# The opening block of a two-layer kernel: one list for its input transfers, and a new place for four weight slots

## Chip, cores and metric

One NeuronCore of one Trainium2 chip. The metric is the device time of one execution in microseconds (us); the profile is one execution of its own.

## The reference, cut to what matters

The reference is two blocks one after the other on 1024 tokens of width 1024, float32. Only its beginning is touched:

```python
c_act = jax.nn.silu(c)
mod = c_act @ ada_w[l] + ada_b[l]                       # 1024 x 6144: sh1, sc1, gt1, sh2, sc2, gt2
h = rms_norm(x, pre1_w[l]) * (1.0 + sc1) + sh1          # norm over the width, for each token
z = h @ w_in[l]                                         # the mixer's projections
...
mem_kv = mem @ w_mem_kv[layer]                          # second block, 256 memory rows, two layers
```

`mem_kv` depends on nothing but inputs, so the kernel computes it in its opening block and puts it into device memory for the second block.

## The kernel before, in words

**Layout.** Activations lie with the width on the 128 partitions, in 8 tiles, and the tokens along the free dimension, in two halves of 512. Each float32 operand of a large product is split into a rounded part (`hi`, fp32r) and the rest (`lo`), and a product is three matmuls (`three`, L285 to L292): w_hi x_hi, w_hi x_lo, w_lo x_hi.

**Weights.** All large weights come as one stream of slots of 128 x 1024 float32 (0.52 MB), in the order of use. A slot is fetched by SP into one of two raw buffers (`raw_w`, `RAW` = 2), rounded on ScalarE (`round_slot`, L268, the instruction L273) and its low part made on GpSimd (`rest_of_slot`, L276, L282) into one of four ring places (`w_hi`, `w_lo`, `RING` = 4). Slot n can be fetched when slot n - 2 has been split (semaphore `w_split`), and rounded when the matmuls of slot n - 4 are done.

**The opening block** (L975 to L1266) runs these parts side by side:

- `modulation` (L993): loads the vectors `vec` and constants `cst`, then 16 slots of `ada_w` (0.52 MB each, 6 buffers, so slot n waits for `ada_done` of slot n - 6). On the tensor engine each takes 8 matmuls (`modulate`, L943). After every four slots the vector engine picks the sums (`pick_group`, L950, L953); after the last it adds the bias and folds the norm's weight in (`folded`, L957).
- `first_slots` (L1041): fetches weight slots 0 to 13, rounds slots 0 to 3 and splits slots 0 to 11.
- `squares` (L1060): loads x in four quarters of 1.05 MB (first the two of token half 0), squares each tile on ScalarE (L1080) and adds them up on the vector engine (L1090).
- `statistic` (L807), once for each half: a reduction over the partitions on the tensor engine (L824), the root on ScalarE (L856), reciprocal (L850) and diagonal (L835) on the vector engine, and a matmul that spreads the factors (L831).
- `normed` (L1094), once for each half: scales x by norm and fold (vector engine, L1105), adds the shift and rounds (ScalarE, L1121, L1124, L1127), and makes the low parts on the vector engine (L1111) and GpSimd (L1136). Its result is H, high and low.
- `memory_keys` (L1150): loads the memory (`memT`, 1.05 MB), splits it (L1198, L1224), forms keys and values of two layers with weight slots 0 to 7 (24 matmuls each), copies them out of PSUM (keys on ScalarE L1204 and L1205, values on the vector engine L1232) and stores them (L1159, L1160). On ScalarE it also rounds slots 4 to 11, each behind the copy of the slot whose ring place it takes. `memT` and its parts lie in the space of H's low part, so the first low tiles of H wait for all eight slots (`kv_t` at 8).
- `heads_in` (`dense`, L607): the first projections from H, weight slots 8 to 12: four outputs for token half 0, the same four for half 1, and a fifth for both; 240 matmuls of 512 columns.

**What sets the order.** Each part is a set of generators, one for each engine; before every piece of work a generator yields a planned time. `ordered` (L137) merges the generators of an engine by these times, and the engine then executes all pieces in that order, each with its semaphore waits: a piece that waits holds everything behind it on its engine. All transfers are issued by SP. The planned times of the old kernel are fixed lines: S(n) = 12 + 2.2 n for modulation slot n, X(i) = 4 + 8 i for quarter i of x, K(n) = 15 + 3.2 n for slot n of the keys and values, N0 = S(16) + 2 for the fold (L988 to L991).

Of the kernel before, what the change touches and what calls it, by code (L numbers as in the profile page):

```python
# [20 lines left out]
F32 = mybir.dt.float32  # L21
# [138 lines left out]
def build(nc, a):  # L160
    ctx = ExitStack()
    with ctx:
# [811 lines left out]
        with ExitStack() as scope:  # L974
# [13 lines left out]
            S = lambda n: 12.0 + 2.2 * n  # L988
            X = lambda i: 4.0 + 8.0 * i
            K = lambda n: 15.0 + 3.2 * n  # L990
            N0 = S(ADA_EARLY) + 2.0  # L991

            def modulation():  # L993
                def on_sp(sp):
                    yield -10.0
                    sp.dma_start(vec[:], a["vec"]).then_inc(loaded.sem, 16)
                    sp.dma_start(cst[:], a["cst"]).then_inc(loaded.sem, 16)
                    for n in range(ADA_EARLY):
                        yield S(n - ADA_RING) + 1.0
                        if n >= ADA_RING:  # L1000
                            sp.wait_ge(ada_done.sem, n - ADA_RING + 1)
                        sp.dma_start(ada_w[:, n % ADA_RING].rearrange("p k m -> p (k m)"), a["ada"][n]
                                     ).then_inc(ada_full[n % ADA_RING].sem, 16)

                def on_pe(pe):
                    for n in range(ADA_EARLY):
                        yield S(n)
# [7 lines left out]
                def on_act(act, link):  # L1015
# [3 lines left out]
                    yield N0  # L1019
# [3 lines left out]
                def on_dve(dve, link):  # L1023
# [5 lines left out]
                    for g in range(ADA_EARLY // 4):  # L1029
                        yield S(4 * g + 4) + 0.6  # L1030
# [8 lines left out]
            split_at = lambda n: 10.5 + 2.6 * n if n < RING else K(n - RING) + 4.6  # L1039

            def first_slots():  # L1041
                def on_sp(sp):
                    for n in range(RING + 8 + RAW):
                        yield -3.0 + 0.1 * n if n < RAW else split_at(n - RAW) + 2.6
                        if n >= RAW:
                            sp.wait_ge(w_split.sem, n - RAW + 1)
                        sp.dma_start(raw_w[:, n % RAW], a["w"][n]).then_inc(w_full[n % RAW].sem, 16)

                def on_act(act, link):
                    for n in range(RING):  # L1050
                        yield split_at(n) - 1.4
                        round_slot(act, None, n, 0)

                def on_pool(pool, link):
                    for n in range(RING + 8):
                        yield split_at(n)
# [3 lines left out]
            def squares():  # L1060
# [3 lines left out]
                def on_sp(sp):  # L1064
                    for i in range(4):
                        yield X(i)
                        where = slice(4 * (i % 2), 4 * (i % 2) + 4), tokens(i // 2)
                        sp.dma_start(x0[:, where[0], where[1]], a["x"][:, where[0], where[1]]).then_inc(x_s[i].sem, 16)

# [4007 lines left out]
```

## Time and profile before

| | us |
|---|---|
| median of 3 runs | 3120.64 |
| lowest and highest | 3118.84, 3120.82 |
| the profiled execution | 3119.04 |
| its span, first to last instruction | 3117.2 |

Some 1.8 us of the profiled execution lie outside its span. The profile's page counts TensorE busy for 2885.4 us (93% of the span), VectorE 1606.1, ScalarE 1065.2 and GpSimd 1037.7. The opening block and its projections are the first 4.4% of the span; the row of busy tenths begins with 6 there, against 9 in nearly all slices behind it.

How to read it: in a timeline each line is one instruction, or several alike (x4) with the time from the first's start to the last's end; in brackets stands how long the engine had been idle and which work released it. PE is TensorE, DVE VectorE, ACT ScalarE, POOL GpSimd. SPq lines are the issues of transfers; such a line ends when it is issued, not when the data has landed.

### The profile page before, as it was taken

How to read it: one execution, taken by the hardware profiler on the slowest of the kernel's cores; microseconds unless marked ns; L12 is line 12 of the kernel's file. 1: busy time of each engine (PE TensorE's matmuls, PEld its weight loads, DVE VectorE, ACT ScalarE, POOL GpSimd, SP SyncE). 2: the span in 40 equal slices, each digit the busy share in tenths (PEclk: the TensorE clock that was granted, in tenths of full speed). 3: DMA queues.
4: the chain of work that ended last, by engine and by line, in shares of the span. 5: the costliest groups of instructions: out<-in, count | busy, mean ns of one | idle time of the engine just before them, and what ended most of it. 6: DMA issues, size and time to landing. Idle time of an engine off the chain costs nothing. (4 is left out here: it accounts for less than half of the span.)

```text
span 3117.2 us, 34782 instructions
## 1 busy us (share of the span) xinstructions
PE 2885.4 (93%) x14150; PEld 2181.5 (70%) x14150; DVE 1606.1 (52%) x1686; ACT 1065.2 (34%) x1474; POOL 1037.7 (33%) x577
## 2 busy tenths in 40 slices
PE   6999999999997989799999999899899998999887
PEld 5777777777775568577888777677566666777555
DVE  4263012325335352665555499633466673749557
ACT  4242222212216122433333344434433441347313
POOL 3232111113432121345555467432233331343102
PEclk8989999999998989899999999999999999999889
DMA  8111114662113343212222653412300002121201
GB/s 300 41 55 55 55 68 135 199 206 82 55 68 129 122 144 119 81 48 87 80 80 81 216 170 129 156 58 75 132 21 21 21 18 78 61 81 34 98 14 55
DMA packets 87618, 290.55 MB, mean 93 GB/s; under 512 B 9009, under 2 KB 13505, under 8 KB 86305
## 3 DMA queue, kind: packets, MB, share of 16 engines
q1 hardware_dynamic: 87458, 288.33, 27.5%
q8 instruction: 112, 1.84, 0.2%
q14 instruction: 48, 0.39, 0.0%
HBM read 223.70 MB, written 64.59 MB: 92 GB/s over the span
## 5 line engine op out<-in xcount | busy, mean ns | idle before, releaser
L282 POOL TENSOR_TENSOR w_lo_sb<-raw_w_sb,w_hi_sb 128x1024 fp32r<-128x1024 f32 x155 | 386.1, 2492 | 1241.2 <-ACT w_hi_sb L273 1241.1
L290 PE MATMUL ps<-h_hi_sb,w_hi_sb 128*128 128x512 f32 x720 | 300.4, 417 | 10.2 <-PEq L537 5.4
L290 PE MATMUL ps<-h_lo_sb,w_hi_sb 128*128 128x512 f32 x720 | 289.4, 402 | 0.0
L290 PE MATMUL ps<-h_hi_sb,w_lo_sb 128*128 128x512 f32 x720 | 251.9, 402 | 0.0
L273 ACT ACTIVATE w_hi_sb<-raw_w_sb 128x1024 fp32r<-128x1024 f32 x155 | 163.3, 1054 | 206.3 <-PE ps L290 155.2
L290 PE MATMUL ps<-z_lo,w_hi_sb 128*128 128x512 f32 x512 | 205.0, 400 | 0.0
L290 PE MATMUL ps<-merged_parts_hi_sb,w_hi_sb 128*128 128x512 f32 x472 | 190.8, 404 | 13.1 <-DVE merged_parts_lo_sb L2775 8.1
L290 PE MATMUL ps<-merged_parts_lo_sb,w_hi_sb 128*128 128x512 f32 x472 | 188.6, 399 | 0.0
L290 PEld LDWEIGHTS ps<-h_hi_sb,w_hi_sb 128*128 128x128 f32 x720 | 138.4, 192 | 55.4 <-issue 22.5
L290 PE MATMUL ps<-merged_parts_hi_sb,w_lo_sb 128*128 128x512 f32 x472 | 176.8, 396 | 0.0
L290 PE MATMUL ps<-z_hi,w_hi_sb 128*128 128x512 f32 x384 | 162.6, 423 | 13.9 <-PEq L912 5.6
L290 PEld LDWEIGHTS ps<-h_hi_sb,w_lo_sb 128*128 128x128 f32 x720 | 138.5, 192 | 34.1
L290 PEld LDWEIGHTS ps<-h_lo_sb,w_hi_sb 128*128 128x128 f32 x720 | 138.8, 193 | 31.2 <-issue 1.0
L290 PE MATMUL ps<-hid_hi_sb,w_hi_sb 128*128 128x512 f32 x308 | 124.2, 403 | 14.6 <-DVE hid_lo_sb L3311 14.6
L290 PE MATMUL ps<-z_hi,w_lo_sb 128*128 128x512 f32 x384 | 133.4, 402 | 0.0
L290 PE MATMUL ps<-h_hi,w_hi_sb 128*128 128x512 f32 x256 | 113.3, 443 | 14.9 <-POOL h_lo L3480 11.6
L3718 PE MATMUL ps<-att_p_t_sb,vh_sb 128*128 128x512 f32 (+3 forms) x288 | 124.2, 513 | 1.6 <-ACT att_p_t_sb L3852 1.6
L3032 POOL TENSOR_TENSOR w_lo_sb<-ffn_weight_sums_sb,w_hi_sb 128x512 fp32r<-128x512 f32 x72 | 105.2, 1465 | 55.3 <-ACT w_hi_sb L2986 55.1
L290 PE MATMUL ps<-hid_hi_sb,w_lo_sb 128*128 128x512 f32 x308 | 122.9, 399 | 0.0
L290 PE MATMUL ps<-hid_lo_sb,w_hi_sb 128*128 128x512 f32 x308 | 122.0, 396 | 0.0
L290 PEld LDWEIGHTS ps<-merged_parts_hi_sb,w_hi_sb 128*128 128x128 f32 x472 | 89.3, 189 | 42.7 <-issue 7.3
L290 PE MATMUL ps<-y_parts_hi_sb,w_hi_sb 128*128 128x512 f32 x224 | 97.6, 436 | 22.4 <-DVE y_parts_lo_sb L2283 8.9
(676 smaller groups left out, 6791.5 us busy)
## 6 DMA issues: line engine op xcount, KB each, us to landing
raw_w_sb<-in_w SPq DMA_DIRECT2D x237, 512.0 KB, 3.6
ada_late_sb<-in_ada SPq DMA_DIRECT2D x32, 512.0 KB
inbox_sb<-gates_out SPq DMA_DIRECT2D x24, 512.0 KB, 4.1
ffn_hidden_out<-ffn_hidden_box_sb SPq DMA_DIRECT2D x22, 512.0 KB, 6.2
ffn_hidden_sb<-ffn_hidden_out SPq DMA_DIRECT2D x20, 512.0 KB, 5.3
ada_w<-in_ada SPq DMA_DIRECT2D x16, 512.0 KB, 8.4
gates_out<-outbox_sb SPq DMA_DIRECT2D x16, 512.0 KB, 2.6
inbox_sb<-sums_out SPq DMA_DIRECT2D x16, 512.0 KB, 5.1
```

The lines of the kernel that those rows point to most:

```text
L273: nc.scalar.activation(w_hi[:, n % RING].rearrange("p t m -> p (t m)"), raw_w[:, n % RAW], ACT.Copy).then_inc(w_rounded.sem, 1)
L282: nc.gpsimd.tensor_tensor(w_lo[:, n % RING].rearrange("p t m -> p (t m)"), raw_w[:, n % RAW], flat_hi, ALU.subtract).then_inc(w_split.sem, 1)
L290: mm = nc.tensor.matmul(o, wt, xs, start=start and part == 0 and xs is x_hi, stop=stop and part == 1, skip_group_check=again)
L3032: nc.gpsimd.tensor_tensor(flat4(half_slot(w_lo, j)), weight_of(g, j), flat4(half_slot(w_hi, j)).bitcast(F32), ALU.subtract).then_inc(split ...
L3718: nc.tensor.matmul(ps[:, 6 + t, lo - HALF * t:HALF], v_of(u, s), pr[n % PR][:, 0:hi - lo], start=(s == 0), stop=(s == last(t))).then_inc(p ...
```

## The change

The planned times come from one list. Each of its 31 transfers is planned to land when the megabytes up to it have passed at 0.39 MB per us, and SP issues it 12 us before that. In the list slots 0 to 7 come early, most of x and the modulation behind them. The lines for S, K, the splits, the fold and the projections are worked out from these landing times. Weight slots 8 to 13 are not in the list: they stay in `first_slots`, at planned times worked out from `split_at`. The roundings of slots 4 to 11 move from `memory_keys` to `first_slots` with planned times of their own, and the wait on `kv_t` with them. The stores of keys and values get later planned times. `memT` gets a buffer of its own, and its two parts move behind the first four low tiles of H, so that the wait for `kv_t` at 8 stands at the low tiles 4 and 5.

```diff
-            S = lambda n: 12.0 + 2.2 * n
-            X = lambda i: 4.0 + 8.0 * i
-            K = lambda n: 15.0 + 3.2 * n
-            N0 = S(ADA_EARLY) + 2.0
+            MB_US = 0.39
+            fetched = [("vec", 0), ("cst", 0), ("w", 0), ("w", 1), ("mem", 0), ("ada", 0), ("w", 2), ("ada", 1), ("w", 3),
+                       ("x", 0), ("w", 4), ("ada", 2), ("w", 5), ("ada", 3), ("ada", 4), ("w", 6), ("ada", 5), ("w", 7),
+                       ("x", 1), ("ada", 6), ("ada", 7), ("x", 2), ("ada", 8), ("ada", 9), ("ada", 10), ("x", 3),
+                       ("ada", 11), ("ada", 12), ("ada", 13), ("ada", 14), ("ada", 15)]
+            megabytes = {"vec": 0.15, "cst": 0.6, "w": 0.524, "mem": 1.05, "ada": 0.524, "x": 1.05}
+            lands, now = {}, 0.0
+            for what, n in fetched:
+                now += megabytes[what] / MB_US
+                lands[(what, n)] = now
+            S, at = [], 0.0
+            for n in range(ADA_EARLY):
+                at = max(lands[("ada", n)] + 0.5, at + 1.3)
+                S.append(at)
+            X = lambda i: lands[("x", i)]
+            K, at = [], 13.0
+            for n in range(8):
+                at = max(lands[("w", n)] + 4.0, at)
+                K.append(at)
+                at += 3.2
+            K.append(at)
+            FOLDED = S[-1] + 4.0
+            H0 = FOLDED + 5.0
...
                 def on_sp(sp):
-                    yield -10.0
...
+                    for what, n in fetched:
+                        yield lands[(what, n)] - 12.0
...
+                        if what == "w":
+                            if n >= RAW:
+                                sp.wait_ge(w_split.sem, n - RAW + 1)
+                            sp.dma_start(raw_w[:, n % RAW], a["w"][n]).then_inc(w_full[n % RAW].sem, 16)
...
-            split_at = lambda n: 10.5 + 2.6 * n if n < RING else K(n - RING) + 4.6
+            split_at = []
+            for n in range(RING + 8):
+                ready = (lands[("w", n)] if n < 8 else split_at[n - RAW] + 4.5) + 1.5
+                split_at.append(max(ready, K[n - RING + 1] + 1.6) if n >= RING else ready)

             def first_slots():
                 def on_sp(sp):
-                    for n in range(RING + 8 + RAW):
-                        yield -3.0 + 0.1 * n if n < RAW else split_at(n - RAW) + 2.6
-                        if n >= RAW:
-                            sp.wait_ge(w_split.sem, n - RAW + 1)
+                    for n in range(8, RING + 8 + RAW):
+                        yield split_at[n - RAW] + 2.6
+                        sp.wait_ge(w_split.sem, n - RAW + 1)
                         sp.dma_start(raw_w[:, n % RAW], a["w"][n]).then_inc(w_full[n % RAW].sem, 16)

                 def on_act(act, link):
-                    for n in range(RING):
-                        yield split_at(n) - 1.4
+                    for n in range(RING + 8):
+                        yield split_at[n] - 1.4
+                        if n >= RING:
+                            act.wait_ge(kv_t.sem, n - RING + 1)
                         round_slot(act, None, n, 0)
...
-                        yield X(i) + 7.0 + 0.8 * (t % 4)
+                        yield X(i) + 0.6 + 1.0 * (t % 4)
...
-                            if n == 2:
+                            if n == 6:
                                 dve.wait_ge(kv_t.sem, 8)
...
-            memT = sb_over("mem_in", [P, DT, MEM], F32, h_lo_at)
-            MT = (sb_over("mem_parts_hi", [P, DT, MEM], F32R, h_lo_at + 8 * T),
-                  sb_over("mem_parts_lo", [P, DT, MEM], F32R, h_lo_at + 16 * T))
+            memT = sb_in(scope, "mem_in", [P, DT, MEM])
+            MT = (sb_over("mem_parts_hi", [P, DT, MEM], F32R, h_lo_at + 16 * T),
+                  sb_over("mem_parts_lo", [P, DT, MEM], F32R, h_lo_at + 24 * T))
...
-                        yield K(4 * layer + 4) + 3.0
+                        yield K[4 * layer + 4] + (22.0 if layer == 0 else 10.0)
...
                             n = 4 * layer + m
-                            yield K(n + 1) + 0.2
+                            yield K[n] + 3.4
                             act.wait_ge(kv_t.sem, n + 1)
...
-                            round_slot(act, None, n + RING, 0)
...
-                at = X(2 * h + 1) + 12.0
+                at = X(2 * h + 1) + 6.0
```

## Rows read from the trace of the kernel before

**Rows 1.** The page's first line, and SP's longest wait of 0 to 85 us (in total, times, longest).

```profile
span 3117.2 us, 34782 instructions
...
SPq L1047 <- POOL w_lo_sb L282: 38.6, 10, 6.6
```

**Rows 2.** Windows: length, PE, PEld, DVE, ACT, POOL busy (instructions), TensorE clock, DMA share, GB/s.

```profile
3.00:10.00 7.00, 0.00 (x0) 0.00 (x0) 3.55 (x6) 0.21 (x1) 0.00 (x0) 1.00 0.99 406
...
40.00:50.00 10.00, 10.00 (x89) 9.67 (x90) 5.05 (x9) 5.96 (x9) 7.30 (x3) 0.78 0.57 179
50.00:60.00 10.00, 10.00 (x122) 8.37 (x121) 1.82 (x4) 2.57 (x5) 2.10 (x2) 1.00 1.01 377
```

**Rows 3.** Timeline of SP: start us, us, what.

```profile
46.98 0.44 SPq L1068 DMA_DIRECT2D x_sb<-in_x  x1
...
48.68 0.44 SPq L1047 DMA_DIRECT2D raw_w_sb<-in_w  x1
```

**Rows 4.** The tile raw_w: splits on POOL, and DMA issue to landing.

```profile
L282 POOL TENSOR_TENSOR w_lo_sb<-raw_w_sb,w_hi_sb x12: 2338/2357/2652, 11.7 to 70.8; 128x1024 fp32r<-128x1024 f32 x12
...
DMA to landing us min/median/max: 3.5/5.1/11.8
```

**Rows 5.** Timeline of ACT (roundings L273, squares L1080, key copies L1204).

```profile
10.23 0.42 ACT L1198 ACTIVATE mem_parts_hi<-mem_in 128x256 fp32r<-128x256 f32 x1 [4.93 <-DMA mem_in<-in_mem]
...
56.85 1.06 ACT L273 ACTIVATE w_hi_sb<-raw_w_sb 128x1024 fp32r<-128x1024 f32 x1 [5.99 <-DMA raw_w_sb<-in_w]
57.94 0.38 ACT L1204 ACTIVATE mem_k_sb<-ps 64x256 f32<-64x256 f32 x1
...
61.97 1.06 ACT L273 ACTIVATE w_hi_sb<-raw_w_sb 128x1024 fp32r<-128x1024 f32 x1 [3.26 <-DMA raw_w_sb<-in_w]
62.93 0.61 ACT L1080 ACTIVATE norm_sq_sb<-x_sb 128x512 f32<-128x512 f32 x1
...
67.36 1.04 ACT L273 ACTIVATE w_hi_sb<-raw_w_sb 128x1024 fp32r<-128x1024 f32 x1
```

**Rows 6.** Timeline of DVE (diagonal L835, sums L1090, pick L950, scaling L1105, low part L1111).

```profile
45.18 1.25 DVE L835 TENSOR_TENSOR norm_diag_sb<-cst_sb,norm_stat_sb 128x512 f32<-128x512 f32 x1
...
63.57 4.81 DVE L1090 TENSOR_TENSOR norm_total_sb<-norm_total_sb,norm_sq_sb 128x512 f32<-128x512 f32 x4 [11.69 <-ACT norm_sq_sb L1080]
...
73.62 0.28 DVE L950 TENSOR_TENSOR ada_pick_sb<-ps,ada_own_row_sb 128x128 f32<-128x128 f32 x1
...
75.04 2.06 DVE L1105 SCALAR_TENSOR_TENSOR x_sb<-x_sb,fold_sb,ps 128x512 f32<-128x512 f32 x3
77.02 0.74 DVE L1111 SCALAR_TENSOR_TENSOR h_lo_sb<-x_sb,mod_sb,h_hi_sb 128x512 fp32r<-128x512 f32 x1
```

**Rows 7.** Timeline of POOL (split).

```profile
63.10 2.34 POOL L282 TENSOR_TENSOR w_lo_sb<-raw_w_sb,w_hi_sb 128x1024 fp32r<-128x1024 f32 x1 [2.73 <-ACT w_hi_sb L273]
```

**Rows 8.** Timeline of PE, start us, us (L943 modulation, L824 reduction, the rest L290).

```profile
14.47 0.42 PE L290 MATMUL ps<-mem_parts_lo,w_hi_sb 128*128 128x256 f32 x1
...
16.82 0.41 PE L290 MATMUL ps<-mem_parts_hi,w_hi_sb 128*128 128x256 f32 x1
...
55.73 0.28 PE L290 MATMUL ps<-w_lo_sb,mem_parts_hi 128*128 128x256 f32 x1
...
58.34 0.28 PE L290 MATMUL ps<-w_hi_sb,mem_parts_lo 128*128 128x256 f32 x1
58.55 0.64 PE L943 MATMUL ps<-ada_w,ada_silu_sb 128*32 128x128 f32 x16
...
68.44 1.87 PE L824 MATMUL ps<-cst_sb,norm_total_sb 128*128 128x1 f32 x8 [5.65 <-DVE norm_total_sb L1090]
70.23 2.79 PE L943 MATMUL ps<-ada_w,ada_silu_sb 128*32 128x128 f32 x48
...
77.86 0.77 PE L290 MATMUL ps<-h_hi_sb,w_hi_sb 128*128 128x512 f32 x1 [2.04 <-issue]
...
136.06 0.63 PE L290 MATMUL ps<-h_hi_sb,w_lo_sb 128*128 128x512 f32 x2
```

More of the change, by code:

```diff
@@ L993, in modulation @@
+            K.append(at)
+            FOLDED = S[-1] + 4.0
+            H0 = FOLDED + 5.0
             def modulation():
                 def on_sp(sp):
-                    yield -10.0
[L996 to L1003, printed above, removed]
+                    for what, n in fetched:
+                        yield lands[(what, n)] - 12.0
+                        if what == "vec":
+                            sp.dma_start(vec[:], a["vec"]).then_inc(loaded.sem, 16)
+                        if what == "cst":
+                            sp.dma_start(cst[:], a["cst"]).then_inc(loaded.sem, 16)
+                        if what == "mem":
+                            sp.dma_start(memT[:], a["mem"]).then_inc(mem_s.sem, 16)
+                        if what == "w":
+                            if n >= RAW:
+                                sp.wait_ge(w_split.sem, n - RAW + 1)
+                            sp.dma_start(raw_w[:, n % RAW], a["w"][n]).then_inc(w_full[n % RAW].sem, 16)
+                        if what == "ada":
+                            if n >= ADA_RING:
+                                sp.wait_ge(ada_done.sem, n - ADA_RING + 1)
+                            sp.dma_start(ada_w[:, n % ADA_RING].rearrange("p k m -> p (k m)"), a["ada"][n]
+                                         ).then_inc(ada_full[n % ADA_RING].sem, 16)
+                        if what == "x":
+                            where = slice(4 * (n % 2), 4 * (n % 2) + 4), tokens(n // 2)
+                            sp.dma_start(x0[:, where[0], where[1]], a["x"][:, where[0], where[1]]).then_inc(x_s[n].sem, 16)
@@ L1194, in on_act @@
                     for t in range(DT):
-                        yield 9.0 + 0.4 * t
+                        yield lands[("mem", 0)] + 0.6 + 0.5 * t
                         if t == 0:
@@ L1206, in on_act @@
                                                  ).then_inc(k_taken.sem, 1)
-                            round_slot(act, None, n + RING, 0)
-                        for part in range(2):
-                            n = 4 * layer + 2 + part
-                            yield K(n + 1) + 0.3
-                            act.wait_ge(kv_t.sem, n + 1)
-                            round_slot(act, None, n + RING, 0)
                 def on_dve(dve, link):
@@ L1221, in on_dve @@
                     for t in range(DT):
-                        yield 9.6 + 0.4 * t
+                        yield lands[("mem", 0)] + 1.2 + 0.5 * t
                         dve.wait_ge(mem_hi.sem, t + 1)
@@ L1226, in on_dve @@
                     for layer in range(2):
-                        yield K(4 * layer + 4) + 0.2
+                        yield K[4 * layer + 3] + 3.4
                         dve.wait_ge(kv_t.sem, 4 * layer + 4)
@@ L1237, in build @@
             for h in range(2):
-                at = X(2 * h + 1) + 12.0
+                at = X(2 * h + 1) + 6.0
                 root = statistic(at, total[:, tokens(h)], [(acc_s.sem, 7 * h + 7)], (2 + h,), D, dg[:, h], st[:, h])
-                parts += [root, normed(h, max(at + 8.0, N0 + 10.0 * h), root.done, 2 + h)]
+                parts += [root, normed(h, max(at + 8.0, FOLDED + 10.0 * h), root.done, 2 + h)]
             act_free.n += 8
```

31 lines of the change are left out of this document (12 added, 19 removed).

## The prediction

> **What bounds the kernel now.** The page gives one core, a span of 3117.2 us [rows 1]. The change touches the first 140 us only, so I read that stretch: the windows, then each engine's timeline, in which the reader looks for what the last wait before the first projection is. From its first `h` matmul at 77.86 us the tensor engine works almost without a gap to 136.06 us [rows 8]: this stage is as long as its matmuls, and what matters is when it begins. Backwards from there: the low parts of `h` follow the first scaling at 75.04 [rows 6], that follows the fold, the fold the last modulation slots (70.23) [rows 8]. Those had landed long before; they stand in the tensor engine's queue behind the norm's second reduction (68.44), that waits for the sums of squares (63.57, four of them [rows 6]), and those for the squares at 62.93, which stand on ScalarE behind the rounding of weight slot 9 at 61.97 [rows 5]. So the chain is transfers, then an order: x's last quarter was issued at the end of a queue that reached 406 GB/s (3 to 10 us) but only 179 GB/s in 40 to 50 [rows 2], because SP stands in order behind waits for splits: 38.6 us in ten waits [rows 1].
>
> **What the change does to the orders.** No arithmetic is added or taken away: 37 input transfers and 4 key and value stores before and after, 12 roundings, 12 splits, 16 modulation slots. Every engine runs its pieces sorted by planned times, so I worked out the planned times from the formulas of the diff and sorted them. Done for the old formulas, the same sorting gives the order that ScalarE's timeline shows: round 9, four squares, round 10 [rows 5]. The new one:
> - SP: the list as written, but slots 8 to 13 aren't in it; slot 8 comes at 27.5 (behind slot 10 of the modulation), slot 9 at 30.2, slot 10 at 33.5, modulation 14 and 15 at 34.3 and 35.6, slot 11 at 36.4. List entries are issued 12 us ahead of their planned landing, so there is a backlog; yet the plan of slot 8's rounding (29.5) assumes 1.9 us from issue to landing.
> - ScalarE: round 8 (29.5), squares 5 and 6 of the first half, round 9, square 7 (32.4), ..., round 10 (35.6), ..., round 11 (38.8), and only then the last quarter's squares (41.5). Before, rounds 10 and 11 came behind these squares.
> - Tensor engine: first reduction (34.8), slot 7 of the keys and values (35.4), modulation 8 (36.0), ..., second reduction (46.9), modulation 15 (48.1).
>
> The chain of waits is thus longer: the last squares now need slot 11 in place of slot 9. Slot 11 is issued behind modulation 14, whose buffer waits for modulation 8, that for the first reduction, that for square 7, and that for slot 9.
>
> **The sum, in us of the trace.** Slots 0 and 1 and the memory (2.85 MB with the two tables) are ahead of the first ScalarE operation at 10.23 [rows 5]; at 406 GB/s the stream starts at 3.2. A 0.52 MB transfer takes 1.3, and the shortest issue to landing is 3.5 [rows 4], so an empty queue costs 2.2 from an issue to the first byte.
> 1. Through slot 9 the queue carries 17.0 MB: 41.9, so 45.1 without gaps.
> 2. Gaps: slot 2 is issued when slot 0 is split (6.2 + 1.06 + 2.36 [rows 4], about 9.7), slot 4 at 16.7: 0.5 each. Slot 4's rounding stands behind the key copy of slot 0 (planned 16.4 against 16.8), whose matmuls begin near 15 at the low clock, 12 matmuls 0.214 apart in [rows 8], so 24 take 5.1, and the DVE's memory parts hold them to 21. Copy, rounding, split: slot 6 is issued at 25.4 into a queue that ran out at 25.4: 2.2. Slot 5's rounding stands behind the second key copy in the same way; slot 7 goes out at 31 instead of 28: 2.9. With these 6.1, slot 9 lands at 51.2.
> 3. Rounding 1.06, key copy 0.76 (two of 0.38 [rows 5]), square 0.6: 53.6. The running sum waits out the GpSimd split, as the four at 63.57 did (4.81 for four, the split at 63.10 lasting 2.34 [rows 6, 7]): 55.4. Reduction 1.8 (68.44 to 70.23): 57.2. Slot 7: 24 matmuls take 2.85 at full clock (23 of them, 0.119 apart [rows 8]) and 5.1 at the low; after an idle stretch I take 4.0: 61.2. Modulation 8, 0.64 [rows 8]: 61.9. Then three transfers into an empty queue: 3.5 + 2 x 1.3, so slot 11 lands at 68.0.
> 4. Rounding and split 3.4: 71.5. Four sums of 0.74 (2.94 for four once the split at 63.10 is over) and a pick of 0.57 between: 75.0. Reduction 1.8, modulation 15 0.93 (2.79 for three [rows 8]), pick to scaling 1.42 (73.62 to 75.04), reciprocal and diagonal 1.3 [rows 6]: 80.5. From the first scaling to the first matmul 2.8 as now (75.04 to 77.86): 83.3.
>
> That is 5.4 later than 77.86, and the stage behind keeps its length, since its weights (slots 8 to 11) are split by 71.5. The profiled execution took 3119.04, 1.6 under the median of the runs, 3120.64; 3119.04 + 5.4 = **3124.4 us**.
>
> Edits costed at nothing: the two key/value stores per layer move to the end (1.6 MB, 4 us of queue, after everything the stage needs; without that cover they would delay slot 12, whose ring place is free only after the fifth of the stage's half outputs). The memory input gets its own buffer and the parts move behind H's first four low tiles, so the wait for all keys and values moves from the first low tile to the fifth: both are met by 61. Roundings 4 to 11 leave memory_keys for first_slots, with the same waits.
>
> **Bounds.** Item 2 is the least sure: the rows of before have no stream in this order. If the key copies don't hold the roundings (full clock from the start), only the two small gaps stay: slot 9 at 46.1; if slots 0 to 2 run wholly at the low clock, 53. Slot 7 is 2.85 to 5.1. The first projection could stay at the low clock for longer: that adds 2.25 to the 24 matmuls of a slot, so an estimated 4.5 to 24 of twice the width, and over half of it is paid now; up to 2 more. Together 0.9 earlier to 11 later: 3118 to 3130. I take 5.4, near the middle.
>
> **A rule that speaks of the queue.** The rows show 406 GB/s in 3 to 10 us, and 377 in 50 to 60 with the queue full [rows 2]; my sum uses 406. The Trainium skill, DMA: Bandwidth & Descriptors, section Specifications, puts HBM at about 358 GB/s for a core. The trace doesn't agree. By that figure item 1 would be an estimated 47.5 instead of 41.9 and the result an estimated 3130.
>
> **Rivals.**
> - **The plan holds, faster.** SP's early waits are short, slots 8 to 11 come as planned, and the queue never empties. All input with slots 8 to 11 is 20.7 MB: 51 us at 406 GB/s, so it is in by 54.2; modulation, pick, fold and scaling as now (from 73.0, the end of the last modulation, to 77.86: 4.9) put the first matmul at about 60. 17 to 18 us less: 3102. For it: the queue is the obvious waste of now (179 GB/s). Against it: the two-slot ring asks for four round trips in a row after slot 8, each behind a backlog, and round 11 stands ahead of the last squares whatever the rate. It decides if rounds 8 to 11 start before 50.
> - **Small transfers overtake the backlog, no change.** If slots 8 and 9 land 5.1 after issue (the median [rows 4]) although 2 to 4 MB is ahead of them, slot 9, issued near 39.4 when slot 7 is split and the backlog lets SP on, lands at 44.5: 6.7 less, 3117.7. Against: slot 8, issued at 48.68 behind x's last quarter [rows 3], made ScalarE wait until 56.85 [rows 5].
> - **The splits hold the memory's parts, slower.** Slots 0 and 1 are now split at 7 to 12, just when the vector engine takes the low parts of the memory, which share the wait seen at 63.57. Each split in the way moves slot 0's matmuls, and with them slots 4 to 7, by 2.4; two beyond my working: +10, 3129 to 3131.
>
> **Chances.** My working 0.68, plan holds 0.12, overtaking 0.08, held parts 0.12. About 0.2% (6.2 us, 3114.4 to 3126.9) is what a measurement of this kernel can tell from no change. Of my own case about 0.28 lies above 3126.9 (its upper bound is 3130), with held parts 0.31 slower; faster are the plan (0.12) and a tail where the plan holds in part (0.04). The range 3113 to 3131 leaves out the first rival and a little on each side.
>
> **What the changed profile would show.** Right: round 9 near 51 us, ScalarE idle before rounds 8 and 11 for several us (for weight DMAs), the tensor engine idle up to about 55 and again to about 75 before the two reductions, SP's issue of modulation 14 near 62, first `h` matmul near 83, and the same 58 us from it to the end of the stage. Wrong: modulation 14 issued before 50, a queue at 400 GB/s through 50 us, last squares ahead of round 11, or a first `h` matmul before 72 or after 90.

## The result: slower, by the chain that the prediction named, and 1.7 us more of it

| us | before | after |
|---|---|---|
| median of 7 runs each, taken on one chip | 3120.82 | 3130.51 |
| lowest and highest | 3118.84, 3128.91 | 3126.72, 3137.33 |
| the profiled execution, its span | 3119.04, 3117.2 | 3131.4, 3129.6 |
| first matmul of the first projection | 77.86 | 84.96 |
| ScalarE's copy of the fifth projection's sums, at the end of the projections (the *marker* below) | 136.72 | 143.77 |

The ratio after to before is 1.0028 [1.0018, 1.0037], slower by some 9 us; a second series (e8 below) gave 1.0022 [1.0012, 1.0031], 7.3 us by the medians. The prediction was 3124.4 in 3113 to 3131; the measured median lies 0.5 below the upper end of that range, and three of the seven runs lie above it.

The last two lines of the table say where it went: the opening block is 7.1 us longer, the first projection as long as before (58.8 us in both). In these two profiles the rest of the kernel is another 5.3 us apart (from the marker to the end 2980.5 before, 2985.8 after); that part is taken up behind the experiments.

**The profile after.** Windows of after; the columns are those of [rows 2].

```profile
10.00:20.00 10.00, 5.75 (x51) 4.71 (x52) 8.93 (x10) 4.68 (x10) 6.91 (x3) 1.00 0.97 324
20.00:30.00 10.00, 10.00 (x117) 9.33 (x117) 4.50 (x6) 5.96 (x11) 4.37 (x2) 1.00 0.91 326
30.00:40.00 10.00, 8.24 (x91) 7.65 (x90) 1.57 (x5) 3.26 (x5) 5.19 (x3) 1.00 0.86 315
40.00:50.00 10.00, 5.41 (x49) 4.79 (x40) 0.00 (x0) 1.26 (x2) 0.12 (x1) 0.77 1.04 402
50.00:60.00 10.00, 3.19 (x15) 3.19 (x16) 5.96 (x7) 5.92 (x10) 5.67 (x3) 0.50 0.59 237
60.00:65.00 5.00, 5.00 (x68) 4.67 (x68) 4.67 (x9) 1.99 (x4) 1.26 (x1) 0.76 0.04 7
```

The list does what it is written to do: 402 GB/s in 40 to 50 us, where before had 179 [rows 2]. Then the queue runs dry: 7 GB/s in 60 to 65. The engines show why. ScalarE's timeline after (roundings L273, squares L1108):

```profile
48.74 1.06 ACT L273 ACTIVATE w_hi_sb<-raw_w_sb 128x1024 fp32r<-128x1024 f32 x1 [11.00 <-DMA raw_w_sb<-in_w]
49.71 1.13 ACT L1108 ACTIVATE norm_sq_sb<-x_sb 128x512 f32<-128x512 f32 x2
52.73 1.06 ACT L273 ACTIVATE w_hi_sb<-raw_w_sb 128x1024 fp32r<-128x1024 f32 x1 [1.89 <-DMA raw_w_sb<-in_w]
...
57.76 1.06 ACT L273 ACTIVATE w_hi_sb<-raw_w_sb 128x1024 fp32r<-128x1024 f32 x1 [2.14 <-DMA raw_w_sb<-in_w]
...
70.24 1.06 ACT L273 ACTIVATE w_hi_sb<-raw_w_sb 128x1024 fp32r<-128x1024 f32 x1 [7.77 <-DMA raw_w_sb<-in_w]
71.20 1.13 ACT L1108 ACTIVATE norm_sq_sb<-x_sb 128x512 f32<-128x512 f32 x2
```

The bracket of round 8 is the thing to see: 11.00 us idle for a weight slot, and the two squares that follow it start the moment it is done, so their x had been there. The same at 70.24 with round 11, 7.77 us, again followed at once by squares. SP's timeline after (L1079 slots 8 and on, L1033 x, L1029 modulation):

```profile
34.59 1.34 SPq L1079 DMA_DIRECT2D raw_w_sb<-in_w  x1
35.98 0.91 SPq L1033 DMA_DIRECT2D x_sb<-in_x  x1
37.69 2.59 SPq L1079 DMA_DIRECT2D raw_w_sb<-in_w  x1
40.32 3.63 SPq L1029 DMA_DIRECT2D ada_w<-in_ada  x3
52.25 0.33 SPq L1079 DMA_DIRECT2D raw_w_sb<-in_w  x1
64.01 0.86 SPq L1029 DMA_DIRECT2D ada_w<-in_ada  x2
64.92 9.15 SPq L1079 DMA_DIRECT2D raw_w_sb<-in_w  x3
```

Slot 8 goes out at 34.59 and its rounding begins 14.2 us later; slot 11 goes out behind modulation 14 and 15. And TensorE's timeline (L824 reduction, L943 modulation):

```profile
56.81 1.86 PE L824 MATMUL ps<-cst_sb,norm_total_sb 128*128 128x1 f32 x8 [10.74 <-DVE norm_total_sb L1118]
...
63.30 1.52 PE L943 MATMUL ps<-ada_w,ada_silu_sb 128*32 128x128 f32 x48
...
77.16 1.87 PE L824 MATMUL ps<-cst_sb,norm_total_sb 128*128 128x1 f32 x8 [8.88 <-DVE norm_total_sb L1118]
78.96 1.08 PE L943 MATMUL ps<-ada_w,ada_silu_sb 128*32 128x128 f32 x16
...
84.96 0.77 PE L290 MATMUL ps<-h_hi_sb,w_hi_sb 128*128 128x512 f32 x1 [0.61 <-issue]
```

Modulation 8 ends near 63.9, and at 64.01 SP sends modulation 14: this is one chain through ScalarE, the vector engine, TensorE and SP. TensorE waits 10.74 and 8.88 us for the sums of the two reductions; for the second it was 5.65 before [rows 8].

### The profile page after: what moved, and what is told of

The parts are those of the page before. It is cut to its first block and busy times, and to the rows that moved or that the text cites. A ratio compares the mean times of both kernels' runs of the same rounds, so it can differ in the third digit from the quotient of the medians.

```text
span 3129.6 us, 34786 instructions
## 1 busy us (share of the span) xinstructions
PE 2891.1 (92%) x14150; PEld 2185.0 (70%) x14150; DVE 1609.9 (51%) x1686; ACT 1065.1 (34%) x1474; POOL 1037.8 (33%) x577
## 5 line engine op out<-in xcount | busy, mean ns | idle before, releaser
L290 PE MATMUL ps<-h_hi_sb,w_hi_sb 128*128 128x512 f32 x720 | 300.0, 417 | 8.5 <-PEq L537 5.4
L290 PE MATMUL ps<-h_lo_sb,w_hi_sb 128*128 128x512 f32 x720 | 288.7, 401 | 0.0
L290 PE MATMUL ps<-h_hi_sb,w_lo_sb 128*128 128x512 f32 x720 | 252.0, 403 | 0.0
L273 ACT ACTIVATE w_hi_sb<-raw_w_sb 128x1024 fp32r<-128x1024 f32 x155 | 163.3, 1054 | 220.2 <-PE ps L290 157.3
L290 PE MATMUL ps<-z_lo,w_hi_sb 128*128 128x512 f32 x512 | 204.9, 400 | 0.0
L290 PE MATMUL ps<-merged_parts_hi_sb,w_hi_sb 128*128 128x512 f32 x472 | 192.4, 408 | 11.4 <-DVE merged_parts_lo_sb L2795 7.2
L290 PE MATMUL ps<-merged_parts_lo_sb,w_hi_sb 128*128 128x512 f32 x472 | 187.5, 397 | 0.0
L290 PE MATMUL ps<-merged_parts_hi_sb,w_lo_sb 128*128 128x512 f32 x472 | 178.2, 399 | 0.0
L290 PEld LDWEIGHTS ps<-h_hi_sb,w_hi_sb 128*128 128x128 f32 x720 | 138.0, 192 | 53.5 <-issue 21.1
L290 PE MATMUL ps<-z_hi,w_hi_sb 128*128 128x512 f32 x384 | 162.5, 423 | 13.9 <-PEq L912 5.6
L290 PEld LDWEIGHTS ps<-h_hi_sb,w_lo_sb 128*128 128x128 f32 x720 | 138.4, 192 | 33.9
L290 PEld LDWEIGHTS ps<-h_lo_sb,w_hi_sb 128*128 128x128 f32 x720 | 138.4, 192 | 31.1 <-issue 1.0
L290 PE MATMUL ps<-hid_hi_sb,w_hi_sb 128*128 128x512 f32 x308 | 124.2, 403 | 14.1 <-DVE hid_lo_sb L3331 14.1
L290 PE MATMUL ps<-z_hi,w_lo_sb 128*128 128x512 f32 x384 | 133.6, 402 | 0.0
L290 PE MATMUL ps<-h_hi,w_hi_sb 128*128 128x512 f32 x256 | 114.2, 446 | 14.5 <-POOL h_lo L3500 11.2
L290 PE MATMUL ps<-hid_lo_sb,w_hi_sb 128*128 128x512 f32 x308 | 122.6, 398 | 0.0
L290 PE MATMUL ps<-hid_hi_sb,w_lo_sb 128*128 128x512 f32 x308 | 122.0, 396 | 0.0
L290 PE MATMUL ps<-y_parts_hi_sb,w_hi_sb 128*128 128x512 f32 x224 | 97.9, 437 | 22.4 <-DVE y_parts_lo_sb L2303 8.9
L290 PEld LDWEIGHTS ps<-merged_parts_hi_sb,w_hi_sb 128*128 128x128 f32 x472 | 89.7, 190 | 40.0 <-issue 7.3
```

The source lines that it names most:

```text
L273: nc.scalar.activation(w_hi[:, n % RING].rearrange("p t m -> p (t m)"), raw_w[:, n % RAW], ACT.Copy).then_inc(w_rounded.sem, 1)
L290: mm = nc.tensor.matmul(o, wt, xs, start=start and part == 0 and xs is x_hi, stop=stop and part == 1, skip_group_check=again)
```

## The experiments

My theory: two links put four late transfers in a row ahead of H. On ScalarE rounds 8 to 11 stand ahead of squares whose data is there, because `split_at` gives such a slot 1.9 us from issue to landing while the list's lead of 12 us keeps a backlog ahead of it; and on TensorE the first reduction stands ahead of modulation 8, so that it holds SP's issue of modulation 14 and, behind it, of slot 11. Rivals: the list's order of early slots costs the time; the stores or the memory's buffer do; or the loss lies behind the opening. Ratios are to the kernel before on the same chip (e1 to e4 share one series, e5 to e8 another, e9 to e11 a third). The edits are cut to what matters. Line numbers are those of after, in e4 and e5 of before.

**e1: round 11 behind the squares.**

```diff
-                        yield split_at[n] - 1.4
+                        yield split_at[n] - 1.4 + (8.0 if n == 11 else 0.0)
```

> The changed kernel with one planned time moved: ScalarE's rounding of weight slot 11 is planned 8 us later, so that it stands behind the four squares of x's last quarter. Order theory: those squares waited for slot 11 (rounded at 70.24) though x was there, so they start right behind the squares before them, near 62 to 64 us instead of 71.2; the second reduction comes near 69 instead of 77.16 and the first h matmul near 77 to 78 instead of 84.96, about 7 us less, and the time comes back to the kernel before (3119 to 3124). Queue theory (the transfers themselves are late and the order only shows it): the first h matmul stays within 2 us of 84.96 and the time stays near 3130. The wait of the first reduction (56.81) and SP's issue of modulation slot 14 (64.01) stay where they are in both.

Median 3121.82, ratio 0.9999 [0.9989, 1.0008]. First `h` matmul 78.96, 6.0 earlier than after (77 to 78 was forecast). The list, the early slots and SP's order are as in after, and the first reduction comes no earlier (57.95); only ScalarE's order at its end is another. From its ScalarE timeline:

```profile
67.49 0.63 ACT L1108 ACTIVATE norm_sq_sb<-x_sb 128x512 f32<-128x512 f32 x1 [0.17 <-DVE norm_total_sb L1118]
72.20 1.06 ACT L273 ACTIVATE w_hi_sb<-raw_w_sb 128x1024 fp32r<-128x1024 f32 x1 [4.08 <-DMA raw_w_sb<-in_w]
```

The last square is over before slot 11 has landed, where in after the last four came behind it.

**e2: the reductions 6 us later in the plan.**

```diff
-                at = X(2 * h + 1) + 6.0
+                at = X(2 * h + 1) + 12.0
```

> The changed kernel with the reductions of both halves planned 6 us later (12 instead of 6 behind the landing of x), so that the first stands behind slot 7 of the keys and values and modulation slots 8 to 10 on the tensor engine. Theory of the long chain: modulation 8 was held by the first reduction (56.81), that held SP's issues of modulation 14 and 15 (64.01) and of weight slot 11 behind them. With the reduction later, modulation 8 runs near 45 to 47, SP issues modulation 14 near 47 and slot 11 as soon as slot 9 is split, near 56; slot 11 is rounded near 62 instead of 70.24, the first h matmul near 77 to 78, 7 us less. Rival (slot 11 is late because of the raw ring of two alone): slot 11 within 2 us of 70, time unchanged near 3130.

Ratio 1.0002 [0.9993, 1.0012], first `h` matmul 78.98. SP's and TensorE's timelines:

```profile
54.76 1.93 SPq L1029 DMA_DIRECT2D ada_w<-in_ada  x2
58.37 10.05 SPq L1079 DMA_DIRECT2D raw_w_sb<-in_w  x3
```

```profile
60.74 2.79 PE L943 MATMUL ps<-ada_w,ada_silu_sb 128*32 128x128 f32 x48
70.93 2.07 PE L831 MATMUL ps<-norm_diag_sb,cst_sb 128*128 128x512 f32 x2 [7.40 <-DVE norm_diag_sb L835]
72.93 1.64 PE L943 MATMUL ps<-ada_w,ada_silu_sb 128*32 128x128 f32 x32
```

Modulation 14 goes out at 54.76 in place of 64.01 and round 11 starts at 64.61 in place of 70.24, though nothing was done to slot 11. I had forecast 47 for modulation 14 and 62 for round 11: until 54.39 SP still stood ahead of it for slot 10, which waits for the split of slot 8. The first matmul gains 6.0 us and not 9, since another order is now last: modulation 14 and 15 stand behind the matmul that spreads the first half's factors (7.40 us of waiting), whose root ScalarE takes only at 68.00, behind round 11 and two squares of the last quarter.

**e3: slots 8 to 11 in the list**, with planned times from their landing there. One place each: slot 8 ahead of x's last quarter, 9 behind it, 10 behind modulation 13, 11 last (the lines of the list and of SP's loop that do this are left out here).

```diff
-                ready = (lands[("w", n)] if n < 8 else split_at[n - RAW] + 4.5) + 1.5
+                ready = lands[("w", n)] + 1.5
```

> The changed kernel with weight slots 8 to 11 put into the list where SP issued them anyway (8 ahead of x's last quarter, 9 behind it, 10 behind modulation 13, 11 at the end), and their splits planned 1.5 us behind the landing that the list gives, so that every planned time counts the queue. The order of the issues hardly moves; the roundings 8 to 11 move behind the squares whose x lands ahead of them. Theory of the wrong planned times: ScalarE no longer waits 11 us ahead of round 8 nor 7.8 ahead of round 11; first reduction near 45 instead of 56.81, second near 60 instead of 77.16, first h matmul near 69 to 72, 13 to 16 us less than in the changed kernel and 6 to 9 less than before: 3111 to 3116. Theory that the splits on GpSimd hold the memory's parts at the start, or that the clock sets the time: first h matmul stays above 80.

Ratio 0.9966 [0.9954, 0.9978], 12.0 us faster than before by the medians; first `h` matmul 69.93. SP and ScalarE in its timeline:

```profile
35.63 1.46 SPq L1025 DMA_DIRECT2D raw_w_sb<-in_w  x1
37.13 0.91 SPq L1033 DMA_DIRECT2D x_sb<-in_x  x1
38.88 2.56 SPq L1025 DMA_DIRECT2D raw_w_sb<-in_w  x1
41.48 3.62 SPq L1029 DMA_DIRECT2D ada_w<-in_ada  x3
53.33 0.33 SPq L1025 DMA_DIRECT2D raw_w_sb<-in_w  x1
53.70 0.91 SPq L1029 DMA_DIRECT2D ada_w<-in_ada  x2
57.32 0.33 SPq L1025 DMA_DIRECT2D raw_w_sb<-in_w  x1
```

```profile
47.21 1.14 ACT L1108 ACTIVATE norm_sq_sb<-x_sb 128x512 f32<-128x512 f32 x2
49.83 1.06 ACT L273 ACTIVATE w_hi_sb<-raw_w_sb 128x1024 fp32r<-128x1024 f32 x1 [1.48 <-DMA raw_w_sb<-in_w]
...
62.99 1.06 ACT L273 ACTIVATE w_hi_sb<-raw_w_sb 128x1024 fp32r<-128x1024 f32 x1 [0.75 <-DMA raw_w_sb<-in_w]
```

Up to 53.33 SP sends the same transfers in the same order as after, about 1.1 us later each, and round 8 starts as late as in after (49.83 against 48.74). But ScalarE does the work that was ready first: 1.48 us idle ahead of round 8 in place of 11.00, and 0.75 ahead of round 11 in place of 7.77. The transfers weren't the loss, the plan of who waits for them was.

**e9: only the planned stretch of these slots made honest.**

```diff
-                ready = (lands[("w", n)] if n < 8 else split_at[n - RAW] + 4.5) + 1.5
+                ready = (lands[("w", n)] if n < 8 else split_at[n - RAW] + 13.0) + 1.5
```

> The changed kernel with one number moved: the planned stretch from one split to the next landing of the same raw buffer is 13 us instead of 4.5 for slots 8 to 11, which is what the queue's backlog makes of it. This plans roundings, splits and the issues of slots 10 and 11 later; slots 8 and 9 are issued as in the changed kernel. Theory of the wrong planned times: square 7 of the first half no longer stands behind round 9, nor the last squares behind round 11: first reduction near 45, SP's issue of modulation 14 near 45 to 50, second reduction near 60, first h matmul 69 to 73, time 8 to 14 us under the changed kernel (3113 to 3121 where it takes 3130). If instead the list positions of slots 8 to 11 are what e3 gained from, the first h matmul stays above 80.

Ratio 0.9987 [0.9976, 0.9997], 5.2 us faster by the medians; first `h` matmul 69.69. The list is the one of after, so it is the planned times and not a place in the list that e3 mended. With them SP's order moves at its end: slots 10 and 11 go out behind modulation 14 and 15 (five modulation slots in a row from 40.61). The gain in time is smaller than e3's although the first matmul comes as early: rounds 10 and 11 are now planned late and done late (62.16 and 69.59, without idle time before them), and the marker is at 130.92 against 128.74 in e3.

**e10: a lead of 4 us in place of 12.**

```diff
-                        yield lands[(what, n)] - 12.0
+                        yield lands[(what, n)] - 4.0
```

> The changed kernel with the list's entries issued 4 us ahead of their planned landing instead of 12, nothing else. By the planned times slot 8 is then issued behind modulation 6 or 7 instead of 10, slot 9 beside x's third quarter and slots 10 and 11 ahead of the last quarter, so that their landing comes nearer to what the plan of the roundings says. Theory (lead against planned roundings): round 8 near 42, round 11 near 56 instead of 70.24, second reduction near 63, first h matmul 69 to 74, time 7 to 13 us under the changed kernel. If a short lead starves the queue, gaps of 1 to 2 us at each wait of SP eat it up and the first h matmul stays above 78.

Ratio 0.9986 [0.9977, 0.9995], 4.7 us faster by the medians, first `h` matmul 73.87. The backlog is the other half of the same mismatch: slot 8 goes out at 34.12, as in after, and is rounded at 43.28 in place of 48.74. The short lead changes SP's order too: slots 10 and 11 go out ahead of x's last quarter (issued at 51.17). Round 11 came at 58.51, where 56 was forecast.

**e4: the memory's own buffer alone,** put into the kernel before (its parts moved, the waits at the low tiles 4 and 5).

> The kernel before with one part of the change alone: the memory input in a buffer of its own, its parts behind H's first four low tiles, the wait for all keys and values at low tiles 4 and 5 instead of 0 and 1. I costed this at nothing, since the keys and values are done at about 62 us and H's low tiles begin at 77: same time within 0.1% (3118 to 3123), first h matmul within 0.5 us of 77.86. If the place of the buffer matters (a wait, another address), more than 2 us either way.

Ratio 1.0003 [0.9992, 1.0014], marker at 137.03 against 136.72: it costs nothing that can be measured.

**e6: after, with the stores planned as before the change.**

```diff
-                        yield K[4 * layer + 4] + (22.0 if layer == 0 else 10.0)
+                        yield K[4 * layer + 4] + 3.0
```

> The changed kernel with the stores of keys and values planned as before the change (3 us behind the last slot of their layer) instead of 22 and 10 us behind it. I costed moving them at nothing. The first pair (0.8 MB, 2 us of queue) then stands ahead of x's last quarter or weight slot 9, and SP waits for layer 0's values there; the second pair isn't in anyone's way. Theory: slot 9 and all that follows up to 2 us later, first h matmul 85 to 88, time 0 to 3 us above the changed kernel; so the later place is worth 0 to 3 us. Rival (the stores' place costs the changed kernel something): first h matmul earlier than 84.

A miss: I had bounded this by 3 us. First `h` matmul 91.61, 5.8 later than in the like run e8. SP's timeline:

```profile
36.56 1.44 SPq L1079 DMA_DIRECT2D raw_w_sb<-in_w  x1
38.12 1.71 SPq L1185 DMA_DIRECT2D mem_k_out<-mem_k_sb  x1
39.88 0.35 SPq L1186 DMA_DIRECT2D mem_v_out<-mem_v_sb  x1
40.28 0.78 SPq L1033 DMA_DIRECT2D x_sb<-in_x  x1
```

The first layer's stores stand ahead of x's last quarter, which goes out at 40.28, against 35.98 in after; round 9 follows at 56.71 (52.98 in e8), round 11 at 76.89 (71.10). So the later place of the stores is a gain in the trace. Yet the median, 3130.05 with ratio 1.0022 [1.0013, 1.0032], is that of e8, 3130.39 with [1.0012, 1.0031]. In the profiles the lead of 5.9 us at the marker has shrunk to 2.3 at the end. Where the rest was given back in the unprofiled runs I can't show.

**e8: after, once more,** beside e5 to e7.

> The changed kernel itself once more, in more rounds and beside the delay above, for the size of its loss. Opening block theory: the loss is what the first h matmul lost, 7.1 us (84.96 against 77.86), ratio 1.0015 to 1.0030 with 1.0023 in the middle, and equal to that of the delayed kernel before within 0.1%. Rival (a part of the 9.7 us of the medians is a second loss in later stages, where the two profiles drifted apart by another 5 us): ratio above 1.0030 and above that of the delayed kernel by more than 0.1%.

3130.39, ratio 1.0022 [1.0012, 1.0031]; first `h` matmul 85.83.

**e5: before, with its first scaling held up** by eight memsets of 128 x 1024 on the vector engine.

```diff
+                    for _ in range(8):
+                        link(nc.vector.memset(idle[:], 0.0))
```

> The kernel before with eight memsets of 128 x 1024 (0.91 us each, 7.3 to 8 in all) put into the vector engine's chain right behind the fold, ahead of the first scaling: nothing but a delay of the first h matmul, from 77.86 to 85 or 86, as late as in the changed kernel. If a delay of the opening block simply moves all that follows, the median rises by 7 to 8 us over the kernel before (ratio 1.0022 to 1.0026) and the stretch from the fifth projection's copy to the end stays within 2977 to 2988 us. If the stages behind lose or regain some of it by themselves (another phase of the tensor clock), the median rises by less than 4 or more than 11.

The delay was larger than meant: each memset took 0.91 us and its link 0.28, so the first `h` matmul came at 89.20, 11.3 later. The time went from 3123.06 to 3133.27, ratio 1.0028 [1.0016, 1.0040], which is 8.7 us by the ratio (5.0 to 12.5) and 10.2 by the medians. So a delay of the first projection reaches the end at 5 us or more of its 11.3, and its full size lies within the interval.

**e7 and e11: orders of my own, under planned times that hold.** Both put slots 8 to 11 in the list, move several slots of the keys and values behind modulation slots and x's first quarters, and plan the reductions at X + 14. e7 has a lead of 3 us at 0.40 MB per us, e11 another order and a lead of 8 at 0.39. The list of e7:

```diff
-            MB_US = 0.39
+            MB_US = 0.4
...
+            fetched = [("vec", 0), ("cst", 0), ("w", 0), ("mem", 0), ("ada", 0), ("ada", 1), ("w", 1), ("x", 0),
+                       ("ada", 2), ("w", 2), ("ada", 3), ("w", 3), ("ada", 4), ("x", 1), ("ada", 5), ("w", 4),
+                       ("ada", 6), ("w", 5), ("x", 2), ("ada", 7), ("w", 6), ("ada", 8), ("ada", 9), ("w", 7),
+                       ("ada", 10), ("w", 8), ("x", 3), ("w", 9), ("ada", 11), ("ada", 12), ("ada", 13), ("ada", 14),
+                       ("ada", 15), ("w", 10), ("w", 11)]
```

> A version meant to beat both: as e3_slots_in_list, with the list reordered (modulation slots earlier, the memory ahead of weight slot 1, x in between, slots 10 and 11 last), issues 3 us ahead of the planned landing instead of 12, 0.40 MB per us, and the reductions planned 14 us behind x. If planned times that count the queue are all that was wrong, the queue stays full to the end, the list is in by about 56 us, and the first h matmul comes between 58 and 65: 12 to 19 us less than before, 3101 to 3109. If short issue leads leave gaps in the queue of 1 us at each wait, it comes near 70 as in e3.

> A second version meant to beat both: slots 8 to 11 in the list, the list reordered once more (weight slots 5, 7 and 9 a little later, modulation 12 to 14 ahead of slot 10), issues 8 us ahead, 0.39 MB per us, the reductions planned 14 us behind x. The queue has more in hand than in e7_new_order, whose first h matmul was at 62.47 but whose first projection then waited 2.3 us at 66 for a low part behind a late split. If the longer lead fills the gaps (290 GB/s from 40 to 50 us there), the first h matmul is between 59 and 63 and the fifth projection's copy between 119 and 124, time 3103 to 3108; if the splits of slots 10 and 11 on GpSimd still collide with the first low parts, equal to e7 within 2 us.

e7: 3108.63, ratio 0.9954 [0.9940, 0.9967]; e11: 3109.35, ratio 0.9956 [0.9943, 0.9969]. Some 14 us faster than before, over 20 than after, and not to be told from each other (e11 was meant to reach 3103 to 3108). First `h` matmul 62.47 and 63.23. Windows of e7, with the columns of [rows 2]:

```profile
10.00:20.00 10.00, 8.99 (x88) 7.61 (x89) 7.28 (x13) 6.19 (x13) 3.10 (x3) 1.00 1.03 404
20.00:30.00 10.00, 9.10 (x110) 7.96 (x112) 5.75 (x10) 5.51 (x10) 4.76 (x3) 1.00 1.03 401
```

After had 324 and 326 GB/s there, while SP waited for the splits of the first slots; with modulation and x between the slots the queue has something to do during a split. In TensorE's timeline of e7 the first matmul of H is held by another late piece, a split:

```profile
62.47 0.76 PE L290 MATMUL ps<-h_hi_sb,w_hi_sb 128*128 128x512 f32 x1 [2.52 <-POOL w_lo_sb L282]
```

**All of them beside each other.** In us, against before: how far the marker moved, the difference of the medians, and the length from the marker to the end of the profiled span.

| | marker | medians | marker to end |
|---|---|---|---|
| before | 0 | 0 | 2980.5 |
| after | +7.1 | +9.7 | 2985.8 |
| e8, the same | +8.0 | +7.3 | 2985.3 |
| e1 | +1.0 | -1.3 | 2986.8 |
| e2 | +3.0 | +0.6 | 2987.9 |
| e3 | -8.0 | -12.0 | 2980.0 |
| e4 | +0.3 | +0.9 | 2977.3 |
| e5 | +11.4 | +10.2 | 2983.4 |
| e6 | +13.9 | +7.0 | 2981.7 |
| e7 | -12.4 | -14.4 | 2980.5 |
| e9 | -5.8 | -5.2 | 2989.6 |
| e10 | -4.0 | -4.7 | 2980.9 |
| e11 | -13.4 | -13.7 | 2977.8 |

The medians follow the marker, one for one within 4 us, but for e6. The last column is 12 us wide, between kernels that are alike behind the marker; e4, whose marker is where before's is, has the shortest. The changed kernel's own second profile, e8, has 2985.3, near the first's 2985.8, so the 5.3 us do return in it; but by the medians of its series the kernel loses 7.3 us for a marker 8.0 later, which leaves nothing for them. The runs don't show the 5.3 us as an effect of the change, and one profile of before doesn't rule it out. What such a step looks like, in windows of after and of before over the same time:

```profile
980.00:1030.00 50.00, 42.04 (x214) 29.03 (x213) 37.20 (x48) 25.49 (x38) 14.03 (x7) 0.86 0.04 11
```

```profile
980.00:1030.00 50.00, 45.33 (x235) 31.15 (x235) 32.52 (x46) 26.11 (x41) 18.10 (x9) 0.97 0.17 54
```

The granted clock is 0.86 there against 0.97. Up to 989 us most of SP's issues are 5 to 7.5 us later than before's, at 1018 us 12.8, and some 11 to 13.5 from there to the end. Why it falls lower in one execution than in another stays open, and so does e6's median.

## Why the prediction was right, and where it was off

**The chain: right.** The trace after has every link that step 3 and 4 named: reduction at 56.81, slot 7's matmuls, modulation 8, SP's modulation 14 at 64.01, slot 11, the last squares, the second reduction, the fold. e1 and e2 each take one link out and win 6 us; e3 and e9 take both and win 15. "Modulation 14 issued before 50, a queue at 400 GB/s through 50 us, last squares ahead of round 11" stood under what would prove it wrong: the queue was at 402 in 40 to 50, but the rest of that sentence didn't come, and a full queue alone, as it turned out, says nothing against the chain. A mark that both cases meet was badly chosen.

**The sizes: 5.4 predicted, 7.1 measured.** Step by step:

| | predicted | measured |
|---|---|---|
| slot 6, slot 7 issued | 25.4, 31 | 25.0, 30.4 |
| 17.0 MB through the queue | 51.2 | 50.6 |
| round 9 | 51.2 | 52.73 |
| first reduction | 55.4 | 56.81 |
| modulation 14 issued | 61.9 | 64.01 |
| round 11 | 68.0 | 70.24 |
| second reduction | 75.0 | 77.16 |
| first scaling | 80.5 | 82.14 |
| first `h` matmul | 83.3 | 84.96 |

The 17.0 MB are read from windows of after:

```profile
0.00:50.00 50.00, 29.41 (x296) 26.48 (x296) 18.56 (x26) 18.77 (x31) 19.29 (x13) 0.95 0.92 335
56.00:57.20 1.20, 0.39 (x2) 0.39 (x3) 0.75 (x1) 0.00 (x0) 0.20 (x1) 0.50 0.06 24
```

335 GB/s over 50 us are 16.75 MB, the rest follows at 0.41 MB per us. Two terms were mis-sized. The first is the split of a transfer's fixed time, in step 2. I put all of the 2.2 us ahead of the first byte and none behind the last, so I read "17.0 MB have passed" as "slot 9 can be rounded". The rounding began 2.1 us after they had passed. The stream itself was 0.6 ahead of my sum, so that 1.5 are left. For slot 8 the stretch is 2.1 as well: its 15.4 MB had passed at 46.6, by windows of 1 us, and its rounding began at 48.74. Not all of it is time behind the last byte. Behind slot 10 nothing else is queued: the rate falls off at 56, a trickle of 24 GB/s goes on to 57.2 (the second line), and the rounding starts at 57.76, 0.6 behind that. So the last bytes of a slot come later than its share of the stream says. At slot 11 the parts can be read apart, from windows of 1 us: modulation 14 is issued at 64.01, 0.14 MB have passed by 66.0, the 1.57 MB of the three transfers by 69.4, and the rounding starts at 70.24, 0.8 later. From issue to rounding that is 6.2, where the sum had 6.1. The Trainium skill, DMA: Bandwidth & Descriptors, section Anatomy of one DMA, says that the fixed cost is "dominated by **completion latency**, not setup latency". It says so of transfers issued from GpSimd; those here are issued by SP. The trace agrees that a part lies behind the last byte; at 0.8 us behind and over 1 ahead it doesn't show that part as the larger. The second term is slot 7's matmuls: 4.0 taken, 4.8 measured (58.53 to 63.30), its matmuls being 0.214 apart, as at the lower clock of 1.2 GHz, until 62.3; the engine had been idle for 10.74 us ahead of the reduction, and the granted clock is 0.50 in 50 to 60 and 0.76 in 60 to 65. The two make 2.3; the stretch from the second reduction to the first matmul gave 0.5 back (8.3 predicted, 7.8 measured).

**The gaps of step 2: the sum right, in part by luck.** Against 406 GB/s the windows above lose 2.0 us in 10 to 20, 2.0 in 20 to 30 and 2.2 in 30 to 40: 6.2, where I had 6.1. But I had put 1.0 of it before 20 (the gaps of slots 2 and 4) and 5.1 behind it. Slots 6 and 7 went out when and for the reason that I gave (the key copies ahead of the roundings), the gaps of slots 2 and 4 were twice as long as I said, and the two errors cancel. The stream also began some 0.7 us ahead of the 3.2 in my sum. SP's waits after, over the first 92 us: line, what it waited for, total, times, longest:

```profile
SPq L1025 <- POOL w_lo_sb L282: 21.5, 6, 6.2
SPq L1079 <- POOL w_lo_sb L282: 17.0, 3, 8.3
SPq L1029 <- PE ps L943: 11.9, 2, 11.4
```

38.5 us for splits, against 38.6 before [rows 1]: the new list moved these waits and in sum removed nothing, and the third line, the wait for modulation 8, is longer than any of them.

**The rate.** 402 GB/s in 40 to 50 and 409 in 50 to 55 in after bear out the 406 of the sum where the queue is full. The 358 GB/s of the Trainium skill, DMA: Bandwidth & Descriptors, section Specifications, don't hold for this core. Another page of the Trainium skill, Perfetto Trace Analysis, section Roofline, has a single active core bounded by its 16 DMA engines at about 435 GB/s; with that the trace agrees, no window of 5 us that I read being over 419.

**What was costed at nothing.** The memory's buffer: right (e4). The stretch behind the first matmul: right (58.8 in both). The moved stores: wrong in the trace. I said that their later place costs nothing; I didn't ask what their old place, under the new plan, would have cost, and that is 5.8 us of the opening (e6). It didn't change the forecast, as the stores are late in both kernels that it compares.

**The rivals.** The plan holds: it would have shown rounds 8 to 11 before 50; of the four only round 8 was (48.74). Yet e7 comes to 62.5 us, near the 60 that I gave it, once the planned times are true; its idea was right and its price in this kernel wrong. Overtaking: refuted by slot 8, issued at 34.59 and rounded at 48.74, and by slot 9, 37.69 and 52.73. Splits that hold the memory's parts: they do, but within my working. DVE and POOL after:

```profile
14.80 5.27 DVE L1244 TENSOR_TENSOR mem_parts_lo<-mem_in_sb,mem_parts_hi 128x256 fp32r<-128x256 f32 x3 [1.02 <-ACT mem_parts_hi L1224]
```

```profile
14.54 2.36 POOL L282 TENSOR_TENSOR w_lo_sb<-raw_w_sb,w_hi_sb 128x1024 fp32r<-128x1024 f32 x1 [2.38 <-ACT w_hi_sb L273]
17.07 2.38 POOL L282 TENSOR_TENSOR w_lo_sb<-raw_w_sb,w_hi_sb 128x1024 fp32r<-128x1024 f32 x1 [0.17 <-ACT w_hi_sb L273]
```

Three parts take 5.27 us and end at 20.07, 0.6 behind the second split, just as the sums at 63.57 took 4.81 [rows 6, 7]. They put slot 0's key copies at 20.81, where step 2 had 21.

**The chances.** The ratio's interval, 1.0018 to 1.0037, lies at the edge of what counts as slower, on which the prediction had put 0.31, against 0.53 for no change. The working with the two terms mended gives 7.7, and 7.1 was measured; both are on the other side of 6.2. A chain whose every unknown I had rounded to "about the middle" had more on its late side than on its early one: the early end needed all gaps to vanish. The terms of the late end, 1.8 for slot 9, 1.1 for slot 7 and 2 for the clock, make 10.3 with the 5.4, and not the 11 that the bounds have.

**From the opening to the time.** The median after, 3130.51, is 6.1 above the forecast. 1.8 of that is where the forecast started: from the profiled execution, 3119.04, and not from the median of before, 3120.82. 1.7 is the opening. The other 2.6 are not pinned to any stage; in the second series the loss was 7.3 and not 9.7, so they may be the spread between series. That 3130.51 still lies in the range owes something to luck.

## What to carry to other kernels

A planned time is a claim about when data is there, and on an engine that works in order a false one costs more than the wait itself: everything ready behind it waits too, and through the buffers that this frees late it reaches the next transfers. If a list of transfers is issued with a lead, everything that is issued behind that backlog lands a backlog later, so small late slots need the lead in their planned times, or a place in the list. Before a stage is reordered it is worth reading, for each engine, what stands ahead of work whose data has landed: here it brought the first projection 15 us forward without moving one early transfer.

## What the runs showed of the hardware

- A slot of 0.52 MB issued into a full queue is rounded 14 to 15 us after its issue (34.59 to 48.74, 37.69 to 52.73), against 3.5 from issue to landing at the shortest [rows 4]. It is rounded about 2 us after all bytes issued up to it have passed (46.6 and 50.6): slots on SP's queue came as if in the order of issue.
- The end of a burst is slow: behind slot 10 the queue drops from 409 GB/s (50 to 55 us) to 24 (56.0 to 57.2), and only then is the slot usable (57.76).
- A full queue slows the issuer too. SP's issue of one slot takes 0.33 us with little ahead of it and 2.59 at 37.69; three modulation slots take 3.63 at 40.32.
- Sums and memory parts on the vector engine (two operands, both from SBUF) hardly move during a GpSimd split: three parts take 5.27 us, of which 4.5 lie beside two splits, and after the split at 53.86 began, one sum took 1.57 where two alone take 1.49. That is why a split's place matters to the norm.
